# Start-up order, first weight units by terms, and slot order in a two-block transformer kernel

## What is computed

```python
for l in range(DEPTH):                                   # 2
    x = x + 0.5 * swiglu(rms_norm(x, ffn1_norm[l]), ffn1_wg[l], ffn1_wu[l], ffn1_wd[l])   # D_FF 2816
    z = rms_norm(x, mix_norm[l]) @ w_in[l]
    ...                                                  # sliding-window attention with sinks; short convolution
    x = x + jnp.concatenate([attn_out, conv_out], axis=-1) @ w_out[l]
    x = x + 0.5 * swiglu(rms_norm(x, ffn2_norm[l]), ffn2_wg[l], ffn2_wu[l], ffn2_wd[l])
return rms_norm(x, final_norm)
```

```python
u = rms_norm_2(h, norm_mix_g)
conv_in, c_q, c_kv, k_rope_raw, gate_logits = split(u @ w_in)
conv_out = conformer_conv(conv_in, ...)     # glu, 31 taps per channel, layer norm, silu, projection
mla_out  = mla_attention(c_q, c_kv, k_rope_raw, cos, sin, ...)   # 8 heads, rope on 32 of 96 columns, causal
merged   = gates[:, :, 0] * conv_out + gates[:, :, 1] * mla_out
h = h + merged @ w_out
h = h + memory_cross_attention(rms_norm_2(h, g), rms_norm_2(mem, g), ...)
h = h + jnp.square(jax.nn.relu(rms_norm_2(h, g) @ w_mlp1)) @ w_mlp2
return rms_norm_2(h, final_norm_g)
```

## Time and profile before

| | value |
|---|---|
| median of 3 runs | 2609.72 us |
| profiled execution | 2611.04 us |
| its span | 2609.2 us |
| mean granted clock of TensorE | 0.998 |
| TensorE (PE) busy | 2571.6 us, 99% |
| weight loads (PEld) busy | 2126.8 us, 82% |
| VectorE (DVE) busy | 1458.6 us, 56% |
| ScalarE (ACT) busy | 944.8 us, 36% |
| GpSimd (POOL) busy | 362.7 us, 14% |
| moved by DMA | 247.21 MB, 95 GB/s |

### The profile page before, as it was taken

The page is one execution under the profiler, slowest core; times in us unless marked ns, Lnnn a source line. Parts: engine busy times, 40 slices in busy tenths (PEclk is TensorE's granted clock), DMA queues, the critical chain, the costliest instruction groups (busy, mean ns, idle before and its releaser), DMA issues.

```text
span 2609.2 us, 32224 instructions
## 1 busy us (share of the span) xinstructions
PE 2571.6 (99%) x11666; PEld 2126.8 (82%) x11666; DVE 1458.6 (56%) x1741; ACT 944.8 (36%) x1376; POOL 362.7 (14%) x301
## 2 busy tenths in 40 slices
PE   7999999999999999999999999999989999999998
PEld 6888888888888888888888888887778888788887
DVE  7444347764443454443676544445888787652443
ACT  4322224432222232222353322223467534441332
POOL 2000111220001100001123000011166221100001
PEclk9999999999999999999999999999999999999999
DMA  4333323233333333333323333334322333233332
GB/s 142 104 96 92 97 77 97 73 105 97 96 94 95 101 94 96 96 94 95 97 65 92 94 97 96 98 92 122 80 64 75 112 95 108 76 110 96 96 98 80
DMA packets 487837, 247.21 MB, mean 95 GB/s; under 512 B 39873, under 2 KB 484550, under 8 KB 487494
## 3 DMA queue, kind: packets, MB, share of 16 engines
q1 hardware_dynamic: 487298, 245.75, 32.8%
q10 hardware_dynamic: 452, 0.32, 0.1%
HBM read 241.84 MB, written 4.19 MB: 94 GB/s over the span
## 4 chain that ended last, share of the span: by engine, by line
PE 84%; DVE 10%; ACT 3%; POOL 2%; issue 1%; DMA 0%; DVEq 0%; ACTq 0%; POOLq 0%
PE bank L663 13%; PE bank L664 13%; PE bank L665 13%; PE psT L663 10%; PE psT L664 10%; PE psT L665 10%; PE psS L664 3%; PE psS L665 3%; PE psS L663 3%; DVE wlo L1689 2%; POOL zc L2458 1%; DVE bank L2016 1%; ACT whi L1231 1%; ACT sc L1315 1%; DVE sc L1842 1%
## 5 line engine op out<-in xcount | busy, mean ns | idle before, releaser
L1689 DVE TENSOR_TENSOR wlo<-raw,whi 128x1024 fp32r<-128x1024 f32 x466 | 634.2, 1362 | 453.2 <-ACT whi L1231 435.8
L663 PE MATMUL bank<-xhi,whi 128*128 128x512 f32 x1736 | 682.0, 393 | 10.3 <-DVE q2l L2027 4.8
L664 PE MATMUL bank<-xlo,whi 128*128 128x512 f32 x1736 | 676.6, 390 | 0.0
L665 PE MATMUL bank<-xhi,wlo 128*128 128x512 f32 x1736 | 676.3, 390 | 0.0
L1231 ACT ACTIVATE whi<-raw 128x1024 fp32r<-128x1024 f32 x463 | 485.4, 1049 | 333.5 <-PE psT L665 316.7
L663 PEld LDWEIGHTS bank<-xhi,whi 128*128 128x128 f32 x1736 | 326.3, 188 | 83.1 <-DVE q2l L2027 6.7
L665 PEld LDWEIGHTS bank<-xhi,wlo 128*128 128x128 f32 x1736 | 326.3, 188 | 68.5
L664 PEld LDWEIGHTS bank<-xlo,whi 128*128 128x128 f32 x1736 | 326.3, 188 | 68.3 <-issue 1.9
L665 PE MATMUL psT<-hhi,wlo 128*128 128x512 f32 x704 | 273.9, 389 | 0.0
L663 PE MATMUL psT<-hhi,whi 128*128 128x512 f32 x704 | 273.9, 389 | 0.0
L664 PE MATMUL psT<-hlo,whi 128*128 128x512 f32 x704 | 273.9, 389 | 0.0
(11 more groups left out here) (483 smaller groups left out, 3370.6 us busy)
## 6 DMA issues: line engine op xcount, KB each, us to landing
raw<-in_ffn_wg SPq DMA_DIRECT2D x88, 512.0 KB
raw<-in_ffn_wu SPq DMA_DIRECT2D x88, 512.0 KB
raw<-in_ffn_wd SPq DMA_DIRECT2D x64, 512.0 KB
raw<-in_w_mlp SPq DMA_DIRECT2D x64, 512.0 KB
raw<-in_w_in SPq DMA_DIRECT2D x53, 512.0 KB
raw<-in_ffn_wd SPq DMA_DIRECT2D x32, 384.0 KB
raw<-in_w_in SPq DMA_DIRECT2D x24, 256.0 KB
raw<-in_w_out SPq DMA_DIRECT2D x11, 512.0 KB
```

Of the source, the lines that this page charges most:

```text
L663: pe.matmul(dest, a, rhs_hi(k), start=start and k == 0, stop=False)
L664: pe.matmul(dest, a, rhs_lo(k), start=False, stop=False)
L665: mm = pe.matmul(dest, b_, rhs_hi(k), start=False, stop=stop and k == tiles - 1)
L1689: dve.tensor_tensor(wlo[:, a:a + UNIT], raw[:, a:a + UNIT], whi[:, a:a + UNIT].bitcast(F32), ALU.subtract).then_inc(s_split, 1)
```

## The change

- **Transfers.** On ACT's queue the norm rows come first. Sinks and positions are issued behind the third early split, and PE waits for one parameter transfer fewer before it transposes them.
- **First units by terms.** `unit_by_terms` does the first two units of every FFN in three passes of eight matmuls: all of `whi` by `xhi`, then `wlo` by `xhi` and `whi` by `xlo` (the other way round in the second unit), each with its own waits. `norm_sum` also waits for x. In the loops the gate unit waits for the scaled gate of a pair before.
- **Squares of the first x.** ACT copies chunks 1 to 3 of x and squares them straight from PSUM, then squares the other five. POOL adds the first three and chunk 0, DVE the other four and the final sum. The third split follows.
- **First pair.** In each FFN the split of one more unit moves ahead of the root on ACT and ahead of Newton's steps on DVE.
- **Rope angles.** DVE's nine operations go; POOL makes the angles in 13 operations of its own once `inv` is ready in the first FFN, beside the loops.
- **Second block.** A split moves ahead of the copies of k's rope rows. In the slots ACT splits before it makes products; DVE takes out slot 0's unit before its split; PE waits for the rope product instead of the low halves; the variance, root and Newton's steps of the layer norm, and PE's sum of squares for it, take other places; taps are dealt out anew (one more before the slots, two fewer in slot 0, one fewer in slot 1, one more each in slots 8 and 10).

```diff
@@ -428,8 +428,8 @@
-        DVE_SHARE = dict(zip(TAP_VISITS, [2, 2, 2, 2, 3, 0] + [4] * 8 + [3, 4, 3, 4, 5]))
-        ADD_SHARE = dict(zip(TAP_VISITS[2:], [2, 2, 2, 3] + [2, 4] + [5, 4] * 5))
+        DVE_SHARE = dict(zip(TAP_VISITS, [2, 2, 2, 2, 3, 1] + [2, 3] + [4] * 10 + [5]))
+        ADD_SHARE = dict(zip(TAP_VISITS[2:], [2, 2, 2, 1] + [3, 5] + [5, 4] * 5))
@@ -457,7 +457,7 @@
-        FIRST = (0, 4, 6, 5, 1, 2, 3, 7)
+        FIRST = (0, 4, 6, 5, 7)
@@ -665,9 +665,37 @@
+            def unit_by_terms(c, q, dest, N, lows_last):
+                def high(k):
+                    pe.wait_ge(s_xh, N * KC + k + 1)
+                    pe.matmul(dest, wcols(whi, c, k), chunk(xhi, k), start=k == 0, stop=False)
+                def weights_low(k, stop):
+                    return pe.matmul(dest, wcols(wlo, c, k), chunk(xhi, k), start=False, stop=stop)
+                def input_low(k, stop):
+                    pe.wait_ge(s_xl, N * KC + k + 1)
+                    return pe.matmul(dest, wcols(whi, c, k), chunk(xlo, k), start=False, stop=stop)
+                pe.wait_ge(s_hi, q + c + 1)
+                for k in range(KC):
+                    high(k)
+                if not lows_last:
+                    for k in range(KC):
+                        input_low(k, False)
+                pe.wait_ge(s_split, q + (c + 1 + RING))
+                for k in range(KC):
+                    mm = weights_low(k, not lows_last and k == KC - 1)
+                if lows_last:
+                    for k in range(KC):
+                        mm = input_low(k, k == KC - 1)
+                mm.then_inc(s_used, 1)
...
+                pe.wait_ge(s_x, (N + 1) * KC)
@@ -679,14 +707,20 @@
-                        ready = (lambda k: pe.wait_ge(s_xl, N * KC + (k + 1))) if first and p == 0 else None
-                        unit(c, q, b(gate_b[p][:, :]), KC, *xk(), ready=ready)
...
+                            unit_by_terms(c, q, b(gate_b[p][:, :]), N, True)
...
+                        else:
+                            if not first and p == 0:
+                                pe.wait_ge(s_gs, f - 1)
+                            unit(c, q, b(gate_b[p][:, :]), KC, *xk())
...
-                        unit(c + 1, q, b(up_b[p][:, :]), KC, *xk())
+                        if first and p == 0:
+                            unit_by_terms(c + 1, q, b(up_b[p][:, :]), N, False)
+                        else:
+                            unit(c + 1, q, b(up_b[p][:, :]), KC, *xk())
@@ -828,7 +862,7 @@
-                    pe.wait_ge(s_first, 16 * PAR1)
+                    pe.wait_ge(s_first, 16 * (PAR1 - 1))
@@ -970,6 +1004,12 @@
+            def conv_square_sums():
+                for j, a in enumerate(ln_sq):
+                    pe.wait_ge(s_lsq, j + 1)
+                    mm = pe.matmul(tap_b, ones[:, :], a[:, :], start=j == 0, stop=j == CC - 1)
+                mm.then_inc(s_ss, 1)
@@ -977,17 +1017,19 @@
-                        pe.wait_ge(h_lo, 1)
+                        pe.wait_ge(h_cp, 1)
+                        pe.wait_ge(h_rp, 1)
...
-                        pe.wait_ge(h_lo, 2 * h + 1)
+                        pe.wait_ge(h_cp, h + 1)
+                        pe.wait_ge(h_rp, h + 1)
...
-                in_unit(*FILL[s])
+                in_unit(*FILL[s], ready=(lambda k: conv_square_sums() if k == 2 else None) if s == LN_VAR + 1 else None)
@@ -1004,11 +1046,6 @@
-                if s == LN_VAR:
-                    for j, a in enumerate(ln_sq):
-                        pe.wait_ge(s_lsq, j + 1)
-                        mm = pe.matmul(tap_b, ones[:, :], a[:, :], start=j == 0, stop=j == CC - 1)
-                    mm.then_inc(s_ss, 1)
@@ -1246,10 +1283,12 @@
                         if first and p == 0:
+                            split(c + 1 + AHEAD, q)
                             root(N)
...
                         act.activation(tmp[p][:, :], tmp[p][:, :], ACT.Silu).then_inc(s_si, 1)
-                        split(c + 1 + AHEAD, q)
+                        if not (first and p == 0):
+                            split(c + 1 + AHEAD, q)
                         act.wait_ge(s_h, f + p + 1)
@@ -1330,8 +1369,6 @@
-            with nc.allow_non_contiguous_dma(reason="positions, the same in each partition"):
-                act.dma_start(pos[:, :], t["positions_2"][0].partition_broadcast(P)).then_inc(s_par2, 16)
@@ -1340,8 +1377,6 @@
-            with nc.allow_non_contiguous_dma(reason="sinks, the same in each partition"):
-                act.dma_start(sink[:, :], t["attn_sink"].rearrange("l h -> (l h)").partition_broadcast(P)).then_inc(s_first, 16)
@@ -1360,11 +1395,18 @@
-            for c in range(1, AHEAD):
-                first_split(c)
+            first_split(1)
+            for j, m in enumerate((1, 2, 3)):
+                act.wait_ge(s_xl, m + 1)
+                act.activation(chunk(x, m), x_b[m], ACT.Copy)
+                act.activation(chunk(sq0, j), x_b[m], ACT.Square).then_inc(s_q7, 1)
...
-                act.activation(chunk(sq0, j), chunk(x, m), ACT.Square).then_inc(s_q7, 1)
+                act.activation(chunk(sq0, 3 + j), chunk(x, m), ACT.Square).then_inc(s_q7, 1)
+            first_split(2)
+            with nc.allow_non_contiguous_dma(reason="sinks and positions, the same in each partition"):
+                act.dma_start(sink[:, :], t["attn_sink"].rearrange("l h -> (l h)").partition_broadcast(P)).then_inc(s_first, 16)
+                act.dma_start(pos[:, :], t["positions_2"][0].partition_broadcast(P)).then_inc(s_par2, 16)
@@ -1448,11 +1490,11 @@
             root(FIRSTN, first_inv, inv6)
+            split(unit_of("a", 0) + AHEAD, 0)
             act.wait_ge(s_kr, 3)
...
                     act.activation(k2h[r:r + ROPE, j * S:(j + 1) * S], tmp[1][NOPE:QK, :], ACT.Copy).then_inc(s_krh, 1)
-            split(unit_of("a", 0) + AHEAD, 0)
             for j in range(QC, QC + KVC):
@@ -1485,11 +1527,9 @@
+                split(unit_of(*FILL[s]) + AHEAD, 0)
...
-                if s == LN_VAR + 1:
-                    root(LNVAR, acc)
-                split(unit_of(*FILL[s]) + AHEAD, 0)
@@ -1499,6 +1539,8 @@
+                if s == LN_VAR + 1:
+                    root(LNVAR, acc)
@@ -1729,10 +1771,13 @@
-                            inverse(N)
+                            variance(N, psO[:, :], D)
+                            split(c + 1 + AHEAD, q)
+                            newton(N, inv)
...
-                        split(c + 1 + AHEAD, q)
+                        if not (first and p == 0):
+                            split(c + 1 + AHEAD, q)
@@ -1885,35 +1930,6 @@
-            def rope_angles(part):
...
-                for j, cst in enumerate((C1, C2, C3)):
-                    dve.wait_ge(s_ro, 3 + j)
-                    dve.scalar_tensor_tensor(r, n, -cst, r, ALU.mult, ALU.add).then_inc(s_ro, 1)
...
-            rope_angles(0)
@@ -1938,20 +1954,29 @@
-            for m in range(1, 4):
-                first_lo(m)
+            first_lo(1)
+            first_lo(2)
+            other_rows()
+            first_lo(3)
...
-            first_lo(4)
-            other_rows()
-            for m in range(5, KC):
+            for m in range(4, KC):
...
-            for m in FIRST[2:]:
+            for m in FIRST[2:4]:
...
+            dve.wait_ge(s_q7, 3)
+            dve.tensor_copy(chunk(x, 7), x_b[7]).then_inc(s_x, 4)
+            for j in range(3):
+                dve.wait_ge(s_q7, j + 6)
+                if j:
+                    dve.wait_ge(s_v7, j)
+                dve.tensor_tensor(chunk(sq0, 4), chunk(sq0, 4), chunk(sq0, 5 + j), ALU.add).then_inc(s_v7, 1)
+            dve.wait_ge(s_v7, 3)
+            dve.wait_ge(s_sq, 4)
+            dve.tensor_tensor(acc[:, :], acc[:, :], chunk(sq0, 4), ALU.add).then_inc(s_sq, 4)
+            split(2, 0)
...
-            split(2, 0)
-            rope_angles(1)
@@ -2112,8 +2137,6 @@
-                if s == LN_VAR + 1:
-                    variance(LNVAR, tap_b, CW, SUMLN)
@@ -2121,12 +2144,16 @@
+                if s == 0:
+                    evict(*FILL[s])
+                if s == LN_VAR + 1:
+                    variance(LNVAR, tap_b, CW, SUMLN)
...
-                if s == LN_VAR + 1:
-                    newton(LNVAR, acc)
...
+                if s == LN_VAR + 1:
+                    newton(LNVAR, acc)
@@ -2137,7 +2164,8 @@
-                evict(*FILL[s])
+                if s:
+                    evict(*FILL[s])
@@ -2431,10 +2459,39 @@
-            for m in range(2, KC):
+            for m in range(2, 4):
...
+            r, n = rope[64:128, :], sqt[64:128, :]
...
+            pool.wait_ge(s_inv, 1)
+            pool.wait_ge(s_gn, 1)
+            pool.wait_ge(s_par2, 16)
+            pool.tensor_scalar(r, pos[64:128, :], fcol[64:128, 0:1], None, ALU.mult).then_inc(s_ro, 1)
...
+            for cst in (C1, C2, C3):
+                pool.wait_ge(s_ro, step)
+                pool.tensor_scalar(acc[64:128, :], n, -cst, None, ALU.mult).then_inc(s_ro, 1)
```

(10 more changed lines are left out.)

38 lines of the change are left out of this document (16 added, 22 removed).

## The result

The changed kernel takes 2594.73 us, the median of four runs (2594.19 to 2595.51), beside 2609.78 for the kernel before: a ratio of 0.9942 with a 95% interval from 0.9927 to 0.9956. The forecast was 2595.3. The profiled execution took 2594.8 with a span of 2593.0, against 2611.04 and 2609.2.

A forecast was written before the change was run, and what follows sets the result against it. PE, busy 2571.6 of 2609.2 us, was taken as the bound, so only its standstill counts. Terms -8.0 + 0.6 - 7.0 = -14.4 gave 2595.3 us against the median; own range 2591.5 to 2599.5, wider 2590 to 2603.

The forecast's parts named there:

- The head: Start of the kernel up to PE's fifth unit and the rope angles: -8.0 us (-9 to -5.5).
- The 0.4 us for the angles on POOL: Head: POOL's 13 rope operations slow DVE's work on the first hidden pieces, so 0.4 us is given back.
- the -6.4: Head's worth if, by the skill's port rule, three DVE operations each wait up to one POOL operation: 2 us more lost.
- The clock rival: Head: the early, broken start holds the clock low over two units; 9.6 us go, the head's gain is lost; chance 0.07.
- The other FFN starts: Three later FFN starts: gaps for `xhi` cost 1.1 us, one wait for `wlo` goes: +0.6 us (0 to +1.5).
- Rival 4: Loops of the four FFNs: the added wait per pair drains PE 40 times, 20 us on top, 2615 us; chance 0.03.
- The second block: Slots and nearby work: less DVE idle time, together -7.0 us (range -3 to -12.3).
- the 1.4 that PE was to win once at the rope product: Second block: PE starting when the rope product is done helps it by up to 1.4 us once, not per head.
- DVE sets the pace: Second block's slots: DVE, busy 19.03 of 21.4 us, paces them, and PE's wait for `q2l` is a symptom.
- the forecast's 4: Second block: `whi` before the products in each slot removes 4 of the 4.3 us that DVE waits for `whi`.
- a first-slot wait near 1 us: Sign in the slots: a wait near 1 us for the rope product in the first slot.
- Rival 1: Slots: DVE still paces them, second block gives only -3 us, total 2600.6 or 2599 against the median; chance 0.20.

The follow-up runs named there:

- nine_more: Changed kernel with first units tile by tile, slot 2's evict before its taps, taps behind head 2's `k2l`, plus DVE's first memset cut into ten: 2592.28 us.
- act_products_first: The changed kernel with ACT making a slot's first tap product ahead of its `whi`, as before the change: 2599.14 us.

## Why the prediction was right

*The head*, forecast 8.0, measured 8.8. That the passes began at 12.53 where 12.5 was forecast is luck, three errors that met. The rows led by 2.9 us, not 1.6: the step took x's landing as nearly unmoved, and x landed 1.7 sooner. Then 1.0 of the 2.9 was lost again, because the transposes ran at half pace until 11.87, about the same moment as in the kernel before. And PE was held not by `whi`, ready at 11.47, but by its own transposes, the last of which started at 12.42 (`cw` was done at 12.18). The sum was ready at 24.72 for 24.4; PE's wait was 1.15 where "a few tenths" and "under 1 us" stood, because its two units took 11.2 us and not 11.9. The fifth unit followed without a gap at 36.93 for 37.2. The 0.4 us for the angles on POOL were not paid: beside the angles PE had no wait, so the -6.4 was not seen either. The slowing itself is there, in DVE's second split, which ran beside POOL's first add; the same operation took 1.21 us alone:

```profile
17.12 2.09 DVE L1731 TENSOR_TENSOR wlo<-raw,whi 128x1024 fp32r<-128x1024 f32 x1
16.83 1.29 POOL L2461 TENSOR_TENSOR acc<-sq 128x512 f32<-128x512 f32 x1 [12.54 <-ACT sq L1402]
```

The Trainium skill's page "SBUF — State Buffer" (the shared port pair) says that such a pair of operations excludes one another for a whole instruction. These two rows agree with it: POOL's add ended at 18.12, 1.21 more is 19.33, and the split ended at 19.21.

The clock rival did not come true in the head. In 3.9 us behind the wait for the sum the granted clock was 1.00, had 0.61:

```profile
24.87:28.77 3.90, 3.90 (x14) 2.65 (x15) 3.90 (x5) 3.48 (x5) 0.00 (x0) 1.00 0.41 112
```

*The other FFN starts*, forecast +0.6, measured +1.3. The waits for `xhi` 7 cost 0.34, 0.48 and 0.34, 1.2 for 1.1, and the wait for `wlo` near 934 went, 0.6 for 0.5. The step missed the waits for `ptlo`, 2 x 0.35 longer; that it comes of the instructions ahead of them on DVE is what nine_more suggests.

*The added wait per pair* cost nothing: no PE gap stands in the loops of the four FFNs. Rival 4 is out.

*The second block*, forecast 7.0, measured 7.1, with the parts off. The terms themselves add up to 6.6, or to 8.0 with the 1.4 that PE was to win once at the rope product; the 7.0 lies between. The units ahead of slot 0 gave 1.2 (7.5 to 8.7) where 0.8 was forecast, and slot 0 gave 4.4 (to 13.1) where 2.5 and up to 1.4 were. There the evict stood behind a split that had itself waited 3.60 us for `whi`. Now it needs only PE, and PE waits for it no more. Before, and after:

```profile
1893.65 0.68 DVE L1983 SCALAR_TENSOR_TENSOR tmp<-bank,inv 128x512 f32<-128x512 f32 x1
1894.38 0.50 PE L856 MATMUL bank<-lath,whi 128*128 128x512 f32 x1 [3.18 <-DVE tmp L1983]
...
1880.46 0.69 DVE L2008 SCALAR_TENSOR_TENSOR tmp<-bank,inv 128x512 f32<-128x512 f32 x1 [1.34 <-PE bank L665]
```

Slots 1 and 2 gave back 2.5: the step took no account of slot 2, where `gate_a` is taken out behind four taps; PE, earlier than before, waited 2.81 for it and ran at a granted clock of 0.58 behind it:

```profile
1905.69 0.50 PE L890 MATMUL bank<-lath,whi 128*128 128x512 f32 x1 [2.81 <-DVE gate_a L2010]
```

```profile
1905.69:1909.80 4.11, 4.11 (x14) 3.63 (x15) 3.35 (x5) 1.95 (x4) 0.24 (x2) 0.58 0.38 97
```

From slot 4 on two slots take 20.25 us instead of 21.4, with PE busy all the time:

```profile
1930.06:1950.31 20.25, 20.25 (x111) 17.48 (x111) 17.46 (x26) 16.10 (x31) 15.86 (x13) 1.00 0.27 66
```

That "DVE sets the pace" and that the place of `whi` is what counts is right, and the ACT order's 3.8 to 5.0 us are about the forecast's 4. But the 4 was to come from DVE's waits for `whi`, and those are mostly still there: 3.4 us in five waits against the 4.3 in nine of the earlier trace rows.

```profile
DVE wlo L1731 <- ACT whi L1268: 3.4, 5, 1.6
```

What changed is how long DVE's splits take. With `whi` earlier, most splits start ahead of POOL's next add and take 1.4 us, and the add takes 2.1; before, most started behind the add and took 2.2, and the add 1.3. Before:

```profile
1945.39 1.29 POOL L2458 TENSOR_TENSOR zc<-zc,sqt 128x512 f32<-128x512 f32 x1
1945.55 2.21 DVE L1689 TENSOR_TENSOR wlo<-raw,whi 128x1024 fp32r<-128x1024 f32 x1 [0.50 <-ACT whi L1231]
```

After:

```profile
1932.93 1.37 DVE L1731 TENSOR_TENSOR wlo<-raw,whi 128x1024 fp32r<-128x1024 f32 x1
1933.36 2.10 POOL L2515 TENSOR_TENSOR zc<-zc,sqt 128x512 f32<-128x512 f32 x1
```

Over the four slots from slot 4 on (1942.02 to 1984.88, then 1930.06 to 1970.57) the six splits took 12.2 us before and 9.7 after, POOL's 18 adds 23.3 and 26.5, and DVE's waits for `whi` only 0.6 less. With the old order of ACT (act_products_first, 1931.54 to 1973.20) the splits take 11.2 and the adds 23.3 again. So the size of this term came right by luck, and its mechanism was for the most part another. Two of the signs that the prediction named did not show: waits for `whi` mostly gone, and a first-slot wait near 1 us (it was 0.20).

The prediction also said that letting PE start at the rope product helps once and not per head; in slot 0 it helped, slot 2 took it back, and per head it is worth 0.24. Rival 1 described slots 8 and 10, which kept up; its mechanism, a bank freed behind taps, was real, but in slot 2. What the new tables, the evict of slot 0 and the earlier split ahead of k's rope rows are worth alone was not tried.

## What to carry to other kernels

When every engine but one has slack, look at the engine that the bound one waits for, and at how long its operations take as well as at its waits. Here DVE's splits took 2.2 us beside POOL's adds and 1.4 ahead of them, and moving one 0.7 us operation on ACT, which decides which of the two comes first, was worth more than the edits to PE's own order that were tried. An earlier start is worth nothing ahead of a wait that something else sets: ask of each wait what ends it next, and whether two waits hang on the same work before moving one. Split a change that has a name from the edits that travel with it; here the named one cost 0.8 us and the whole won 15.
